# Splitting the dense weights once and reloading the pairs, in a two-layer streaming encoder on one core

## The reference, cut to what matters

```python
for layer in range(DEPTH):                       # DEPTH = 2
    mod = c @ w_ada[layer] + b_ada[layer]        # adaLN shift, scale, gate from the conditioning
    shift, scale, gate = split(mod, 3)
    h = rms_norm(x, norm_g[layer]) * (1.0 + scale) + shift
    if layer % 2 == 0:
        q, k, v, g_a, u, g_s = split(h @ w_in_even)
        q, k = rope(q), rope(k)
        o_a = attention over the own and the two previous chunks of 64 frames, 8 heads, 2 kv heads, with sinks
        o_s = ssm_branch(u, ...)                 # 32 groups, 64 complex states, then gelu, w_glu, sigmoid gate
        out = concat([o_a * silu(g_a), o_s * silu(g_s)]) @ w_out_even
    else:
        b_g, c_g, hv, g_c = split(h @ w_in_odd, 4)
        yc = short_conv(c_g * hv, conv_w)        # three taps
        out = (silu(g_c) * b_g * yc) @ w_out_odd
    x = x + gate * out
y = rms_norm(x, final_g)                         # also returned: new k, v, SSM states, conv rows
```

## Time and profile before

| what | value |
|---|---|
| runs: median, lowest, highest | 2474.95, 2474.92, 2479.42 us (3 runs) |
| profiled execution, first to last instruction | 2461.4 us |
| the median over that span | 13.5 us |
| PE busy | 2238.7 us, 91% |
| PE's weight loads | 1722.2 us, 70% |
| DVE busy | 875.0 us, 36% |
| ACT busy | 696.1 us, 28% |
| POOL busy | 937.4 us, 38% |
| mean granted TensorE clock | 0.937 |
| DMA | 239.97 MB, mean 97 GB/s |

### The profile page before, as it was taken

One profiled execution on the slowest core, in us unless ns is written; L12 is line 12 of the kernel. 1 busy time (PEld: TensorE's weight loads), 2 busy tenths in 40 slices (PEclk: granted clock), 3 DMA queues, 4 the chain that ended last, 5 costly groups with the idle time before them and its releaser, 6 DMA issues. The chain is left out here.

```text
span 2461.4 us, 28843 instructions
## 1 busy us (share of the span) xinstructions
PE 2238.7 (91%) x10996; PEld 1722.2 (70%) x10996; DVE 875.0 (36%) x1542; ACT 696.1 (28%) x1230; POOL 937.4 (38%) x532
## 2 busy tenths in 40 slices
PE   7778899899977998999888998999898989899997
PEld 1247767688766756887767666887786766688876
DVE  7334352422335453223334533223341253422232
ACT  1132333222322432222313432223212432212121
POOL 0044404355526204555426124555425102333333
PEclk9888999899988998999989998999978989899998
DMA  7754302333242312332262223232431202122221
GB/s 274 224 183 126 120 27 97 102 101 95 86 138 86 120 41 79 120 98 90 69 175 87 73 77 103 94 98 74 151 90 43 95 9 69 52 74 72 70 68 49
DMA packets 77166, 239.97 MB, mean 97 GB/s; under 512 B 11796, under 2 KB 12852, under 8 KB 76628
## 3 DMA queue, kind: packets, MB, share of 16 engines
q1 hardware_dynamic: 62016, 208.54, 26.6%
q10 hardware_dynamic: 15012, 29.56, 4.3%
HBM read 217.61 MB, written 15.02 MB: 95 GB/s over the span
## 5 line engine op out<-in xcount | busy, mean ns | idle before, releaser
L412 POOL TENSOR_TENSOR w_lo<-ring,w_hi 128x1024 fp32r<-128x1024 f32 x264 | 640.3, 2427 | 1305.2 <-ACT w_hi L406 1305.2
L584 PE MATMUL bank<-p_hh,w_hi 128*128 128x512 f32 x1952 | 793.9, 407 | 71.5 <-POOL w_lo L412 43.2
L585 PE MATMUL bank<-p_hl,w_hi 128*128 128x512 f32 x1952 | 781.3, 400 | 0.0
L586 PE MATMUL bank<-p_hh,w_lo 128*128 128x512 f32 x1952 | 780.2, 400 | 0.0
L406 ACT ACTIVATE w_hi<-ring 128x1024 fp32r<-128x1024 f32 x264 | 279.4, 1059 | 1055.0 <-PE bank L586 684.3
L584 PEld LDWEIGHTS bank<-p_hh,w_hi 128*128 128x128 f32 x1952 | 376.4, 193 | 185.8 <-issue 43.2
L586 PEld LDWEIGHTS bank<-p_hh,w_lo 128*128 128x128 f32 x1952 | 376.4, 193 | 82.2
L585 PEld LDWEIGHTS bank<-p_hl,w_hi 128*128 128x128 f32 x1952 | 377.1, 193 | 79.3 <-issue 0.7
L1572 DVE SCALAR_TENSOR_TENSOR p_x<-bank,mod,p_x 128x512 f32<-128x512 f32 x64 | 48.0, 751 | 290.6 <-PE bank L586 290.6
L1667 DVE TENSOR_TENSOR pp_mem<-p_sw,bank 128x512 f32<-128x512 f32 x32 | 22.0, 688 | 325.9 <-PE bank L586 325.9
L533 PE MATMUL bank<-ring,vecs 128*2 128x512 f32 x192 | 91.5, 629 | 29.3 <-DMA ring<-in_ada 29.3
(11 more groups left out here) (301 smaller groups left out, 2511.4 us busy)
## 6 DMA issues: line engine op xcount, KB each, us to landing
ring<-in_dense SPq DMA_DIRECT2D x280, 512.0 KB, 3.5
ring<-in_ada SPq DMA_DIRECT2D x48, 512.0 KB, 4.7
ring<-ssm_scratch SPq DMA_DIRECT2D x48, 512.0 KB, 4.2
p_x<-in_x ACTq DMA_DIRECT2D x4, 2048.0 KB, 12.0
y<-p_g ACTq DMA_DIRECT2D x4, 2048.0 KB, 10.2
u_rows<-in_x ACTq DMA_DIRECT2D x3, 2048.0 KB, 11.0
ssm_scratch<-p_g SPq DMA_DIRECT2D x2, 2048.0 KB, 8.9
p_g<-p_ut ACTq DMA_DIRECT2D x16, 256.0 KB, 13.5
```

What stands on the lines that cost most here:

```text
L412: pool.tensor_tensor(lo, ring[:, slots[name][0], :], hi.bitcast(F32), ALU.subtract).then_inc(split, 1)
L584: pe.matmul(o, ah, bh, start=first, stop=False)
L585: pe.matmul(o, ah, bl, start=False, stop=False)
L586: return pe.matmul(o, al, bh, start=False, stop=last)
```

## The change

The ring shrinks to two slots for raw dense chunks (NRAW = 2; during the preparation two pieces of `prompt.H` serve as slots three and four for w_ada). A new tile `pair` has five places (NPAIR = 5) of two chunks, 1 MB each: a place holds the hi and lo parts of one split chunk, or two chunks that are used as they are (xr and xi of a half, intra and cout of an index, two glu chunks). There are 74 such pairs in a block.

In block one SP loads each raw chunk, ACT and POOL split it as before and at the same spots of their order, now into the pair's place, and SP stores the pair to `parts_scratch` in DRAM (`store_parts`, three items later in its queue). From block two on `split_hi` and `split_lo` return at once, and SP loads whole pairs from DRAM (`load_pair`). A place is reused when the pair five before is used by PE and, in block one, stored. The glu chunks are copied from DRAM to DRAM ahead of block one, so that two of them can be fetched as a pair.

The hardware loop is gone on all engines: blocks one to four are written out. The splits of the next block's u chunks at the end of a block are gone. The clearing of one column of H moves behind the last w_ada product. Several semaphores of the preparation are merged, and so are two pairs of the streams' semaphores; DMAs of x, rope and y have constant addresses.

```diff
-NSLOT = 4
-NSPLIT = 2
+NRAW = 2
+NADASLOT = 4
+NPAIR = 5
...
-        ring = sb("ring", [P, NSLOT, SLOT])
-        w_hi = sb("w_hi", [P, NSPLIT, SLOT], F32R)
-        w_lo = sb("w_lo", [P, NSPLIT, SLOT], F32R)
+        ring = sb("ring", [P, NRAW, SLOT])
+        pair = sb("pair", [P, NPAIR, 2, SLOT], F32R)
...
+        def wait_free(eng, blk, name, streams):
+
+            n = (blk - 1) * len(PAIRS) + PAIR_OF[name] - NPAIR
+            if n < 0:
+                return
+            b, before = n // len(PAIRS) + 1, PAIRS[n % len(PAIRS)]
+            if not by_dma(b, n % len(PAIRS)):
+                eng.wait_ge(parts_out[n % NPAIR], 16 * stores_before(blk, name))
+            for S, sb_ in streams(b):
+                S.wait_used(eng, sb_, before[1] if isinstance(before, tuple) else before)
 
         def split_hi(act, blk, name, streams):
 
+            if blk > 1:
+                return
             n = SPLIT.index(name)
-            for S, b in streams:
-                S.wait_used(act, b if n >= NSPLIT else b - 1, SPLIT[n - NSPLIT])
-            act.activation(parts(name)[0], chunk(act, blk, name), ACT.Copy).then_inc(rounded, 1)
+            wait_free(act, blk, name, streams)
+            act.wait_ge(raw_in[n % NRAW], 16 * (ada_per_slot + n // NRAW + 1))
+            act.activation(parts(blk, name)[0], ring[:, n % NRAW, :], ACT.Copy).then_inc(rounded, 1)
...
+            for i in range(4):
+                sp.dma_start(glu_scratch[i], w_dense[DENSE.index(f"glu{i}")]).then_inc(kt_moved, 16)
...
+            def load_raw(n):
+
+                if n >= NRAW:
+                    sp.wait_ge(split, n - NRAW + 1)
+                sp.dma_start(ring[:, n % NRAW, :], w_dense[DENSE.index(SPLIT[n])]).then_inc(raw_in[n % NRAW], 16)
+
+            def store_parts(n):
+
+                sp.wait_ge(split, n + 1)
+                s = place(1, SPLIT[n])[0]
+                sp.dma_start(parts_scratch[n], pair[:, s, :, :].rearrange("p a m -> p (a m)").bitcast(F32))\
+                    .then_inc(parts_out[s], 16)
...
+                sp.dma_start(pair[:, s, :, :].bitcast(F32), src).then_inc(pair_in[s], 16)
+
+            for i, held in enumerate(PAIRS + [None] * 3):
+                if isinstance(held, tuple):
+                    load_pair(1, held)
+                elif held:
+                    load_raw(SPLIT.index(held))
+                if i >= 3 and not isinstance(PAIRS[i - 3], tuple):
+                    store_parts(SPLIT.index(PAIRS[i - 3]))
+            for blk in range(2, NBLK + 1):
+                for held in PAIRS:
+                    load_pair(blk, held)
...
-            with pe.Fori(1, NBLK) as blk:
-                run_block(blk, lambda b: [(prompt, b)])
-            run_block(NBLK, lambda b: [(prompt, b), (sample, 1)], last=True)
+            for blk in range(1, NBLK + 1):
+                run_block(blk, streams_of, last=blk == NBLK)
```

More of the change, by code:

```diff
@@ L351, in encoder @@
         S.norm = [(S.x, S.sq, S.sum, S.diag)] * 3
-        slot_in = [sem(f"slot{i}_loaded") for i in range(NSLOT)]
+        raw_in = [sem(f"raw{i}_loaded") for i in range(NADASLOT)]
+        pair_in = [sem(f"pair{i}_loaded") for i in range(NPAIR)]
+        parts_out = [sem(f"pair{i}_stored") for i in range(NPAIR)]
         ada_used = sem("ada_chunks_used")
@@ L384, in encoder, with place @@
         NCONST = 16 * 9
-        def chunk(eng, blk, name):
[L388 to L399, removed]
+        def place(blk, name):
+            n = (blk - 1) * len(PAIRS) + PAIR_OF[name]
+            return n % NPAIR, n // NPAIR
@@ new lines, in by_dma, with loads_before, wait_pair @@
+        def by_dma(blk, i):
+            return blk > 1 or isinstance(PAIRS[i], tuple)
+        def loads_before(blk, name):
+            s, k = place(blk, name)
+            return sum(by_dma(*((n * NPAIR + s) // len(PAIRS) + 1, (n * NPAIR + s) % len(PAIRS))) for n in range(k))
+        def wait_pair(eng, blk, name):
+            if by_dma(blk, PAIR_OF[name]):
+                eng.wait_ge(pair_in[place(blk, name)[0]], 16 * (loads_before(blk, name) + 1))
+            else:
+                eng.wait_ge(split, SPLIT.index(name) + 1)
@@ new lines, in chunk, with parts, stores_before @@
+        def chunk(eng, blk, name):
+            wait_pair(eng, blk, name)
+            held = PAIRS[PAIR_OF[name]]
+            return pair[:, place(blk, name)[0], held.index(name), :].bitcast(F32)
+        def parts(blk, name):
+            s = place(blk, name)[0]
+            return pair[:, s, 0, :], pair[:, s, 1, :]
+        def stores_before(blk, name):
+            s, k = place(blk, name)
+            return k - loads_before(blk, name) if blk == 1 else \
+                sum(n % NPAIR == s and not by_dma(1, n) for n in range(len(PAIRS)))
@@ L411, in split_lo @@
-            hi, lo = parts(name)
-            pool.tensor_tensor(lo, ring[:, slots[name][0], :], hi.bitcast(F32), ALU.subtract).then_inc(split, 1)
+            if blk > 1:
+                return
+            n = SPLIT.index(name)
+            pool.wait_ge(rounded, n + 1)
+            hi, lo = parts(blk, name)
+            pool.tensor_tensor(lo, ring[:, n % NRAW, :], hi.bitcast(F32), ALU.subtract).then_inc(split, 1)
         def ut(S, t):
@@ L455, in _ @@
             for i in range(2, NADA):
-                s = i % NSLOT
+                s = i % NADASLOT
                 if i == 20:
@@ L588, in split_chunk @@
             def split_chunk(blk, name, k=KT):
-                wait_split(pe, blk, name)
-                return [weights(x, k) for x in parts(name)]
+                wait_pair(pe, blk, name)
+                return [weights(x, k) for x in parts(blk, name)]
             def project(blk, name, streams, ready=None):
@@ L1254, in run_block @@
                     inverse_root(S, b, 2)
-                if not last:
-                    for name in ("u2", "u3"):
-                        split_lo(pool, blk + 1, name)
             for S, b in ((sample, 1), (prompt, 0)):
@@ L1268, in _ @@
                 split_lo(pool, 1, name)
-            with pool.Fori(1, NBLK) as blk:
-                run_block(blk, lambda b: [(prompt, b)])
-            run_block(NBLK, lambda b: [(prompt, b), (sample, 1)], last=True)
+            for blk in range(1, NBLK + 1):
+                run_block(blk, streams_of, last=blk == NBLK)
         @block.vector
@@ L1748, in _ @@
                     scale(S, b, 0, k)
-            with dve.Fori(1, NBLK) as blk:
-                run_block(blk, lambda b: [(prompt, b)])
-            run_block(NBLK, lambda b: [(prompt, b), (sample, 1)], last=True)
+            for blk in range(1, NBLK + 1):
+                run_block(blk, streams_of, last=blk == NBLK)
 def _layout(inputs):
```

176 lines of the change are left out of this document (84 added, 92 removed).

## The result

The changed kernel takes 2398.53 us, the median of five runs (2389.43 to 2402.71). The kernel before, run beside it, takes 2474.92 (2470.51 to 2479.42). The ratio is 0.9689, 95% interval 0.9668 to 0.9710: 76 us faster, where 99 were forecast.

A forecast was written before the change was run, and what follows sets the result against it. PE's matmul pace was taken as fixed, its idle and half-clock time as winnable: 50 + 14 + 6 + 8 + 13 + 7 + 8 + 8 = 114, less 12 and 3, gives 99; 2475 - 99 = 2376 us, range 2350 to 2418.

The forecast's parts named there:

- R2: Rival, chance 0.15: recurrence or half clock doesn't yield, only half of (a) comes back; 2401 us.
- R1: Rival, chance 0.19: block one becomes bound by transfers in its row of 48 projections, 36 us instead of 12; 2406 us.
- (b): k and v at block start, no longer behind k's split: 6.9 us each in blocks two and three, 14 together.
- glu copies: Before block one: four memory-to-memory copies cost 0 to 6 us, taken as 3.
- block one's traffic: Stores of pairs beside loads in block one: cost between 0 and 36 us, taken as 12.
- (a): SSM input product to last ga projection, blocks two to four: splits gone, gains 15.0, 14.2 and 21 us, together 50.
- (c): SSM weights: PE's waits for their loads go, since five places load far ahead; 5.8 us, summed as 6.
- (d): Norms and gates, blocks without splits: out0's norm 8 us, gates before out1 13, block ends 7.
- part 2: Loop written out: late starts removed twice on PE, 5 us, plus 3 of half clock; 8 us.
- Block one's step ahead: Block one's recurrence and projections: five places let q0 and q1 be split while v runs; gain 8 us.
- The pairs: Pair loads, blocks two to four: 60% of DMA engines, at most 6.3 us issue to landing; cost taken as 0.
- R3: Rival, chance 0.06: pairs land one after another, 6.3 us each against 5.45, in blocks two to four; 2544 us.

The follow-up runs named there:

- e7: Changed kernel with VectorE's sums and rotation of q0 moved ahead of the sample stream's recurrence in block four: 2393.54 us, ratio 0.9690.
- e11: e9 with q1's pair load held until u has landed and q1's rotation ahead of the sample's recurrence: 2348.22 us, ratio 0.9504.
- e3: Changed kernel with each pair load of blocks two to four cut to 64 of 1024 columns of each part: 2383.44 us, ratio 0.9648.
- e1: Changed kernel with the 2 MB load of x issued on ACT behind u's four DMAs instead of ahead: 2372.89 us, ratio 0.9596.
- e9: Kernel of e1 with q0's projection moved ahead of the transposes of u in every block: 2354.08 us, ratio 0.9523.
- e5: Changed kernel with 58 of block one's 66 pair stores left out, all loads kept at their size: 2386.16 us, ratio 0.9652.
- e6: Changed kernel with four places for pairs instead of five: 2396.29 us, ratio 0.9684.
- e4: Kernel before the change with only the hardware loop written out for blocks one to three: 2467.07 us, ratio 0.9984.
- e8: Changed kernel with the edits of e1 and e7 together and each move of u issued behind its own copy: 2372.43 us, ratio 0.9597.
- e12: The same kernel as e1, run again as ground for later runs: 2374.23 us, ratio 0.9598.
- e10: Kernel of e1 with q0's pair load held in blocks two to four until u's moves have landed: 2371.74 us, ratio 0.9583.
- e2: Changed kernel with each stored pair as two planes, so pieces are 4 KB instead of 8 KB: 2391.53 us, ratio 0.9678.

## Why the prediction was right, and where its sizes were off

The forecast was 2376, the range 2350 to 2418, and the result lies in it, 22 us over the forecast. By its number alone it lies nearer to R2 (2401) and R1 (2406) than to the forecast. Neither happened, as the stretches show; the largest part of the difference is a step that no rival named, in (b). By stretches, all blocks together, forecast and measured gain of the span:

| stretch | steps of the prediction | forecast | measured |
|---|---|---|---|
| launch to block one | glu copies | -3 | 1.0 |
| block start to transposes of u | (b), less block one's traffic | 14 - 12 = 2 | -10.7 |
| transposes of u to those of y | (a), (c), block one | 50 + 6 + 8 = 64 | 56.5 |
| from there to the first c | (d), out0's norm | 8 | 5.9 |
| first c to the block's or launch's end | (d) gates 13, ends 7, part 2's 8 | 28 | 21.3 |
| sum | | 99 | 74.0 |

**(a), blocks two and three: right.** 15.6 and 14.4 us against 15.0 and 14.2, down to PE's own time, with one projection 5.45 us as said. The first step of DVE's recurrence takes 0.20 us in block two (750.23), as forecast. R2, half of (a), didn't come.

**(a), block four: 13.3 us instead of 21.** The own time was well estimated at 60: 68.3 us less the wait of 4.79 and less 4.8 of half clock (an estimate, 0.07 x 68.3 at clock 0.93) leaves 58.7. What failed is "That also removes the 7.7 us wait for the sample rotation". DVE's timeline behind the prompt's scans, and POOL's at the same time:

```profile
1782.74 6.64 DVE L1548 TENSOR_TENSOR p_H<-work,p_ut 64x1024 f32<-64x1024 f32 x2
1789.42 2.28 DVE L1550 TENSOR_TENSOR p_last<-work,p_ut 128x16 f32<-128x16 f32 x1
...
1794.15 0.68 DVE L1508 TENSOR_TENSOR p_t<-bank,p_rope 128x512 f32<-128x512 f32 x1
...
1795.89 0.19 DVE L1508 TENSOR_TENSOR s_t<-bank,s_rope 128x32 f32<-128x32 f32 x1 [0.92 <-ACT s_sw L982]
```

```profile
1785.03 6.62 POOL L1246 TENSOR_TENSOR p_H<-pp_mem 64x1024 f32<-64x1024 f32 x2
```

Without splits DVE and POOL reach their two writes of H together, and each pair takes 6.6 us; in the kernel before DVE's took 2.47 in this block, while POOL stood waiting for a split's first half. The 128x16 step behind it takes 2.28 instead of 0.19. Together the two steps took 6.3 us longer, more than the 4.79 of the wait. POOL's two writes took 4.85 us alone and 6.62 beside DVE's. With the splits the offset between the two engines went too, and the rotation's wait stayed for another reason. The Trainium skill ("SBUF — State Buffer", section "SBUF: two separate sides") calls the port pair of VectorE and GpSimd an exclusive lock, held for the whole instruction; the trace agrees, 6.64 us against 2.47. No run here keeps the two engines apart again, so this cause is argued from the timelines. e7 and e11 take back 2.5 us of the wait by order alone.

**(b): the step that failed.** "Both come earlier, so I expect the DMAs by v's end." k and v did start without a split: in block two v was done 40.1 us into the block, before 47.6. But u's moves were issued only 3.3 us earlier (24.0 us into the block, before 27.3), because they follow PE's u products and ACT's copies of them, and from there to the end of PE's wait it took 26.6 us, before 23.4: the 2 MB of x was ahead of them on ACT's queue, as before, and now the pairs were beside it. So PE went on 50.5 us into the block where it had gone on at 50.7, and the u wait, risen from 3.15 to 10.40 us, took (b)'s gain whole. It is also the prediction's own sign of being wrong, "a grouping of u that waits for its DMAs", and it keeps blocks two and three at 503.7 and 505.6 us where "near 496" was said. e3, with thin pairs, has the start of block two at 43.4 us, what (b) forecast (50.7 - 6.9 = 43.8). The sum priced the pairs by their own pace and by block one's u, and put their effect on the u moves of blocks two and three at nothing. e1 gives 0.9 per cent, 23 us, back (0.9596 against 0.9689), and e9 covers what is left. Nor could the 12.2 us of rows 3 have fallen with earlier DMAs: they were DVE's copies nearly whole.

**Block one's traffic, 12 us.** Near in size, 9.9 at its start; in place the prediction hedged between start and row. e5 puts 6.8 of it on the stores, all at the start; e1 shows that with x behind u the start takes 48.2 us, as before the change, stores and all. R1 fell: the row of 48 runs as fast at 283 GB/s.

**Block one's step ahead, 8 us.** From the transposes of u to those of y 9.1 us came. e6 shows that it is the fifth place's doing, and that the place costs as much again ahead of it (11.3 us at the start).

**(c) and out0's norm.** The SSM waits are gone. Out0's norm gave 5.9 against 8.

**Gates, ends, loop: 21.3 against 28.** Before out1 1.98 us of waiting stayed where 1.4 was assumed, and nothing is seen of the 2 us of half clock per block: from the first c to out1 only 1.1 to 1.5 us came in a block, and block four gave 0.9. The stretch from out1 to the next block gave 5.2, 7.2 and 4.0, about as forecast. e4 leaves the loop's own share between 0 and 8 us.

**The pairs: right.** 4.8 us from issue to landing in the median against a bound of 6.3, and no wait of PE for the slower ones. R3 fell with it. The Trainium skill's 6.15 us for 1 MB ("DMA: Bandwidth & Descriptors", section on measured bandwidth) is of transfers issued from GpSimd, and is not what these loads from SP's queue took; the measurement decides.

**The margin** between median and span, 13.5 us, is not the start and end of the launch, as the prediction has it. One execution's time and its own span differ by 2.0 us (2389.43 and 2387.4 in the changed kernel); the rest of the margin is that the profiled execution of the kernel before was quicker than the median. That of the changed kernel was quick as well, 9 us under the median, so the two nearly cancel, by luck: the medians differ by 76 and the spans by 74.0.

## What to carry to other kernels

When a change takes work off one engine, list what else that engine issues in the same stretch, its DMAs first: a large transfer with time to spare (x is read 200 us later, at out0) may have stood ahead of a small one on the critical path without harm until the queues beside it filled up, and one moved line gives the time back. Ask also what sets the moment at which the small one can be issued; that need not move with the rest. A wait on a round trip through memory is better covered with a step of independent work (q0, 5.45 us, gave 20 us, all of it in blocks two to four) than shortened: issuing earlier showed no gain (e8). And an engine's slowness may have kept two engines apart; see who meets whom once it is gone.

## What the runs showed of the hardware

TensorE ran a piece of a stretch without idle time at half clock, in one block and not in the next. The windows show the glu projections of one launch (e12), in block two and in block three, the same matmuls, PE busy from end to end. The last wait ahead of each is one of 1.04 us in attention, 5 us before. In block two the granted clock is 0.50 from 850.34 to 857.17, from the last transpose of y into the glu matmuls.

```profile
850.70:881.70 31.00, 31.00 (x74) 14.16 (x74) 10.27 (x15) 5.84 (x9) 0.00 (x0) 0.90 0.09 34
1356.00:1383.80 27.80, 27.80 (x72) 12.69 (x73) 10.24 (x15) 5.84 (x9) 0.00 (x0) 1.00 0.11 38
```

Which block is hit changes with the run (block three in e1, two in e12 of the same kernel, both in e6 and e10), and a hit costs 3.2 us in these four, more than several of the edits tried here; in e2, e5, e8, e9 and e11 the glu matmuls of one block took 1.4 to 1.7 us longer than in the others. A step worth 3 us is therefore to be read at its own stretch, not in the launch.

The size of a transfer's pieces, 8 or 4 KB, changed neither its own landing (4.8 and 4.9 us) nor what runs beside it (24.8 and 24.2 us for x). The Trainium skill ("DMA: Bandwidth & Descriptors", section "Queues, rings and completion order") says that an engine takes turns between the queues by packets; if a turn were a piece, smaller pieces on SP's queue should have sped up ACT's, which no wait here shows.
